# Hyena filters made ahead of the first norm, and half of them beside the second layer's norm, in a two-layer hybrid backbone on one core

## What is computed

```python
for l in range(DEPTH):                                   # DEPTH = 2
    ml = (silu(c) @ w_mod[l] + b_mod[l])                 # 6 modulation vectors of 1024, for c and c_ctx
    hl = modulate(rms_norm(xl, norm1_g[l]), ml[0], ml[1])
    p = hl @ w_in[l]                                     # one wide input projection
    # three mixers: neighbourhood attention, pooling, and the order-2 Hyena:
    #   hh = sin(freq * (z @ w1 + b1)); hh = sin(freq * (hh @ w2 + b2))
    #   hh = (hh @ w3).reshape(n, 2, 2, 512) * decay      (order, forward/backward)
    #   buf = concat(forward, 0, reversed backward); buf /= sum(abs(buf)); spectrum = rfft(buf)
    #   z = gate_o * irfft(rfft(z) * spectrum_o), for order o = 0, 1
    # merged by gates, projected, gated residual
    # then norm, router, top-2 of 16 experts, gated residual:
    xl = xl + ml[5] * f
out = rms_norm(xl, final_g)
```

## Time and profile before

| | us |
|---|---|
| median of three runs | 1842.62 |
| lowest, highest | 1838.25, 1848.77 |
| the profiled execution | 1845.94 |
| its span in the trace | 1844.2 |

### The profile page before, as it was taken

How to read it: one execution, slowest core, us unless ns; L and a number is a source line. 1 busy time by engine, 2 the same in 40 slices (tenths; PEclk the granted TensorE clock), 3 DMA queues, 4 the chain that set the end, 5 groups by cost and what they waited for, 6 DMA issues and landing times. The chain is left out here.

```text
span 1844.2 us, 19309 instructions
## 1 busy us (share of the span) xinstructions
PE 1546.9 (84%) x7556; PEld 1071.5 (58%) x7556; DVE 819.1 (44%) x1204; ACT 605.2 (33%) x830; POOL 357.9 (19%) x206
## 2 busy tenths in 40 slices
PE   5898997789999977999999766789889987777872
PEld 1365676556666646788888334468678973222322
DVE  2621666751111245889899444144853433000102
ACT  2322222351111242787877124122242331000002
POOL 0132332112222301101010112335124540000000
PEclk8799999799999986999999787889899997999996
DMA  7456321102242305899999722753205446999992
GB/s 247 134 206 239 124 65 52 43 1 69 68 137 68 114 25 217 323 405 405 408 407 368 292 87 83 295 183 99 73 10 179 161 138 229 420 421 422 422 398 80
DMA packets 118416, 374.29 MB, mean 203 GB/s; under 512 B 8222, under 2 KB 70880, under 8 KB 87360
## 3 DMA queue, kind: packets, MB, share of 16 engines
q1 hardware_dynamic: 107584, 334.58, 48.1%
q0 software_dynamic: 10752, 38.61, 5.5%
HBM read 356.39 MB, written 16.78 MB: 202 GB/s over the span
## 5 line engine op out<-in xcount | busy, mean ns | idle before, releaser
L587 POOL TENSOR_TENSOR w_lo<-ring,w_hi 128x1024 fp32r<-128x1024 f32 x120 | 288.7, 2418 | 724.0 <-ACT w_hi L1328 724.0
L705 PE MATMUL bank<-h_hi,w_hi 128*128 128x512 f32 (+1 forms) x896 | 329.8, 368 | 35.3 <-DVE h_lo L1609 21.2
L706 PE MATMUL bank<-h_hi,w_lo 128*128 128x512 f32 (+1 forms) x896 | 311.6, 348 | 0.0
L707 PE MATMUL bank<-h_lo,w_hi 128*128 128x512 f32 (+1 forms) x896 | 311.5, 348 | 0.0
L705 PEld LDWEIGHTS bank<-h_hi,w_hi 128*128 128x128 f32 x896 | 176.3, 197 | 84.9 <-issue 44.6
L706 PEld LDWEIGHTS bank<-h_hi,w_lo 128*128 128x128 f32 x896 | 177.0, 198 | 23.2 <-issue 5.0
L707 PEld LDWEIGHTS bank<-h_lo,w_hi 128*128 128x128 f32 x896 | 176.2, 197 | 20.2
L1328 ACT ACTIVATE w_hi<-ring 128x1024 fp32r<-128x1024 f32 x120 | 125.2, 1052 | 107.9 <-DMA ring<-in_w_in 76.1
L705 PE MATMUL bank<-w_hi,h_hi 128*128 128x512 f32 (+1 forms) x384 | 142.1, 370 | 9.8 <-DVE w_lo L1880 5.1
L1857 DVE SCALAR_TENSOR_TENSOR mix<-mix,bank 128x512 f32<-128x512 f32 (+1 forms) x48 | 26.6, 554 | 262.3 <-PE bank L985 165.4
L706 PE MATMUL bank<-w_hi,h_lo 128*128 128x512 f32 (+1 forms) x384 | 138.8, 362 | 0.0
(11 more groups left out here) (260 smaller groups left out, 2326.9 us busy)
## 6 DMA issues: line engine op xcount, KB each, us to landing
ring<-in_w_up_e SPq DMA_DIRECT2D x54, 1024.0 KB, 8.2
ring<-in_w_in SPq DMA_DIRECT2D x52, 1024.0 KB, 7.0
mix<-in_w_gate_e SPq DMA_DIRECT2D x52, 1024.0 KB, 8.4
ring<-in_w_mod SPq DMA_DIRECT2D x48, 1024.0 KB, 7.2
mix<-in_w_down_e SPq DMA_DIRECT2D x34, 1024.0 KB, 8.9
ring<-in_w_down_e SPq DMA_DIRECT2D x30, 1024.0 KB, 7.8
ring<-in_w_branch SPq DMA_DIRECT2D x12, 1024.0 KB, 5.2
ring<-in_w_gate_e SPq DMA_DIRECT2D x12, 1024.0 KB, 8.6
```

The source lines that it names most:

```text
L587: pool.tensor_tensor(w_lo[:, slot], rview(raw, 8)[:, :, x * P:(x + 1) * P], w_hi[:, slot].bitcast(F32), ALU.subtract).then_inc(w_l, 1)
L705: first = mm(dst, stat[0], mov[0], start=start, stop=False)
L706: mm(dst, stat[1], mov[0], start=False, stop=False)
L707: return first, mm(dst, stat[0], mov[1], start=False, stop=stop)
```

## The change

In the first layer the six tables that the filters need (`c_cols` and `par0` among them) are loaded first, with their own semaphore; `square` and `xT` follow, then the transform tables and the decay with a third semaphore, `s_lds`. TensorE makes `filter_in(0, 0)`, `filter_in(0, 1)` and `filters(0, 0)` ahead of the norm's sums. Then come the eight modulation chunks with `spectra_a(0, 0)` after the fourth, then the transposes of the modulation rows, and `spectra_b(0, 0)` behind them. The products of order 1 use bank 5 in place of bank 7 and have work areas of their own in the second layer (`late_fpm`, `late_fraw`, `late_fhid`). `spectra_a(0, 1)` comes after tile 1, `spectra_b(0, 1)` after tile 2.

Between the layers only order 0 is made ahead of the combination of expert rows; ScalarE takes the rows first and `spectrum_b` after them, and TensorE transposes the modulation rows ahead of `spectra_b`. `filters(1, 1)` stands ahead of the second layer's norm, `spectra_a(1, 1)` behind its sums, `spectra_b(1, 1)` after tile 0 of the projection; on VectorE `taps(1, 1)` stands ahead of the mean.

The diff, cut to its core:

```diff
-        fbank = [bank[i] for i in (2, 3, 4, 7)]
+        fbank = [[bank[i] for i in (2, 3, 4, x)] for x in (0, 5)]
...
-            for dst, name in ((cc[:, 0, :], "c_cols"), (square[:], "square"), (par[0][:], "par0"),
-                              (xT[:], "x_cols")):
-                sp.dma_start(dst, a[name]).then_inc(s_ld, 16)
...
+                if l == 0:
+                    sp.dma_start(cc[:, 0, :], a["c_cols"]).then_inc(s_ldf[l], 16)
+                    sp.dma_start(par[0][:], a["par0"]).then_inc(s_ldf[l], 16)
+                for dst, src in ((fz[l], a["filter_in"]), (fw1[l], a["hy_w1"][l]), (fw2[l], a["hy_w2"][l]),
+                                 (w3s[l], a["hy_w3"][l])):
                     sp.dma_start(dst, src).then_inc(s_ldf[l], 16)
                 if l == 0:
+                    sp.dma_start(square[:], a["square"]).then_inc(s_ld, 16)
+                    sp.dma_start(xT[:], a["x_cols"]).then_inc(s_ld, 16)
+                    sp.dma_start(dft_f[:], a["dft_f"]).then_inc(s_lds, 16)
+                    sp.dma_start(nyq[:], a["nyq"]).then_inc(s_lds, 16)
+                sp.dma_start(decay[l], a["decay"]).then_inc(s_lds, 16)
...
-            pe.wait_ge(s_ld, 16 * 4)
-            norm_pe(0, NT)
...
             def filters(l, o):
                 if o:
-                    pe.wait_ge(f_d[l], 10 * l + 6)
+                    pe.wait_ge(m_tk[l], 3 * l + 1)
                     pe.wait_ge(f_a[l], 6 * l + 4)
                 else:
                     pe.wait_ge(f_a[l], 6 * l + 2)
-                    pe.wait_ge(n_a, l + 1)
...
             def spectra_b(l, o):
                 pe.wait_ge(f_d[l], 10 * l + 5 + 4 * o)
+                if l == 0 or o:
+                    pe.wait_ge(n_a, 2 * l + 1)
...
-            def filters_and_mod(l):
-                filter_in(l, 0)
-                for k in range(DK):
+            def mods_and_filters(l, ks):
+                for k in ks:
                     mod(l, 0, k)
-                    if k == 1:
+                    if k == 1 and l:
                         filter_in(l, 1)
-                    elif k == 3:
+                    elif k == 3 and l:
                         filters(l, 0)
-                    elif k == 5:
+                    elif k == (5 if l else 3):
                         spectra_a(l, 0)
+                mod_columns(l, 0)
                 spectra_b(l, 0)
-                mod_columns(l, 0)
-                filters(l, 1)
+            filter_in(0, 0)
+            filter_in(0, 1)
+            filters(0, 0)
+            pe.wait_ge(s_ld, 16 * 2)
+            norm_pe(0, NT)
             pe.wait_ge(s_cs, 1)
-            filters_and_mod(0)
+            pe.wait_ge(s_lds, 16 * 3)
+            mods_and_filters(0, range(DK))
+            filters(0, 1)
...
                 if l:
+                    filters(l, 1)
                     norm_pe(2 * l, NT)
+                    spectra_a(l, 1)
...
-                    if l == 0 and g == 0:
+                    if l == 0 and g == 1:
                         spectra_a(l, 1)
-                    elif l == 0 and g == 1:
+                    elif g == (0 if l else 2):
                         spectra_b(l, 1)
...
-                    filters_and_mod(l + 1)
-                    spectra_a(l + 1, 1)
-                    spectra_b(l + 1, 1)
-                    pe.wait_ge(f_a[l + 1], 6 * l + 12)
-                    pe.wait_ge(f_d[l + 1], 10 * l + 20)
+                    filter_in(l + 1, 0)
+                    mods_and_filters(l + 1, range(DK))
+                    pe.wait_ge(f_a[l + 1], 6 * l + 10)
                     pe.wait_ge(m_tk[l + 1], 3 * l + 4)
...
                 for k in range(DK):
+                    if k == DK - 1 and l + 1 < DEPTH:
+                        pe.wait_ge(f_d[l + 1], 10 * l + 16)
...
-            act.wait_ge(s_ld, 16 * 4)
+            act.wait_ge(s_ldf[0], 16 * 6)
             A(cc[:, 1, :], cc[:, 0, :], ACT.Exp, scale=-1.0).then_inc(s_ce, 1)
-            norm_act_root(0, NT, 2)
             filter_sin(0, 0)
             filter_sin(0, 1)
+            act.wait_ge(s_ld, 16 * 2)
+            norm_act_root(0, NT, 2)
             spectrum_a(0, 0)
-            spectrum_b(0, 0)
             mod_rows(0, 0)
...
                 if l:
                     norm_act_root(2 * l, NT, 2)
+                    spectrum_a(l, 1)
+                else:
+                    spectrum_b(l, 0)
...
-                    act.wait_ge(z_r, 1)
-                    spectrum_b(l + 1, 0)
-                    spectrum_a(l + 1, 1)
-                    spectrum_b(l + 1, 1)
                 for j in range(nt):
                     act.wait_ge(z_g[j], 32 * (l + 1))
                     A(fa[:, j, :], fa[:, j, :], ACT.Copy, scale=wsel[:, 0, j:j + 1]).then_inc(z_s[l], 1)
+                if l + 1 < DEPTH:
+                    act.wait_ge(z_r, 1)
+                    spectrum_b(l + 1, 0)
...
             def taps(l, o):
                 dve.wait_ge(f_p[l], 8 * l + 3 + 3 * o)
+                dve.wait_ge(s_lds, 16 * (3 + l))
...
-            norm_dve_mean(0, NT)
             angle(0, 0)
-            norm_dve_root(0, NT)
             angle(0, 1)
             taps(0, 0)
-            gate_scales(0, 0)
+            norm_dve_root(0, NT)
             mod_first(0)
...
                 if l:
+                    taps(l, 1)
                     norm_dve_root(2 * l, NT)
                 norm_dve_scale(2 * l, NT)
                 if l == 0:
+                    gate_scales(0, 0)
                     taps(0, 1)
-                    gate_scales(0, 1)
...
+                    if g == (0 if l else 2):
+                        gate_scales(l, 1)
...
                     taps(l + 1, 0)
-                    gate_scales(l + 1, 0)
                     mod_first(l + 1)
-                    taps(l + 1, 1)
-                    gate_scales(l + 1, 1)
...
+                if l + 1 < DEPTH:
+                    gate_scales(l + 1, 0)
```

More of the change, by code:

```diff
@@ L755, in spectra_a @@
                     for j in range(2):
-                        mm(bank[2 + f][:], dft_f[:, j, f * P:(f + 1) * P], fpm[l][:, 0, j, :],
+                        mm(bank[2 + f][:], dft_f[:, j, f * P:(f + 1) * P], fpm[l][o][:, 0, j, :],
                            start=j == 0, stop=j == 1)
                 for j in range(2):
-                    last = mm(bank[4][0:1, :], nyq[:, j:j + 1], fpm[l][:, 0, j, :], start=j == 0, stop=j == 1)
+                    last = mm(bank[4][0:1, :], nyq[:, j:j + 1], fpm[l][o][:, 0, j, :], start=j == 0, stop=j == 1)
                 last.then_inc(f_p[l], 1)
```

41 lines of the change are left out of this document (20 added, 21 removed).

## The result

| | before, us | after, us |
|---|---|---|
| median (six runs each, side by side) | 1844.49 | 1830.29 |
| lowest, highest | 1838.25, 1848.77 | 1827.18, 1832.04 |
| the profiled execution | 1845.94 | 1831.84 |
| its span | 1844.2 | 1830.1 |

The ratio is 0.992, 95% interval 0.9898 to 0.9943: 14.2 us less. Forecast were 31 us less and 1800 to 1828; the measured median lies above that range. The direction was right, the size was not. What came is near rival 1, the cold start (1826).

What follows compares the result with a forecast made beforehand. Chains of short engine handovers ahead of both layers' input projections were taken as the bound. Savings of 12 us in the first layer and 18.7 (28.7 - 3.3 - 6.7) later gave 31, from 1842.62 to 1812, range 1800 to 1828.

Steps and rivals of the forecast that it cites:

- rival 1: Filters, norm, modulation and spectra in both layers run at TensorE's lower clock: gain only 17 us, time 1826; chance 0.14.
- The combination moves: Between the layers, combining expert rows ahead of the second spectrum starts the transposes at 1070.9 instead of 1099.61: 28.7 us less.
- Rival 2: Between the layers, something unnamed holds ScalarE or the gathered rows until 1090, so the combination stays: 1841 us; chance 0.04.
- The stall after tile 0 goes: First layer's projection: TensorE's 3.17 us wait for the second filter's taps and 1.5 us of slow clock disappear.
- What is late next in the first layer: The last modulation chunk's load, not the filters, becomes late: the eighth chunk lands at 52 to 56 us.
- The step from the columns at VectorE at about 56 to the first scaling at about 62.5: First layer: `spectra_b` (1.9 + 3.68 us) and its copies precede scaling, which starts 7.5 us earlier, bounds 4 and 10.
- That the second filter's products run beside the first scalings as before: First layer: these products, 3.6 to 7.2 us on TensorE, overlap the first scalings, as in the kernel before.
- `filters(1, 1)` ahead of the norm: Second layer: 3.6 us of products at the higher clock delay the mean by 3.3 us, bounds 3 and 8.
- `spectra_b(1, 1)` after tile 0: Second layer's projection: its products and ScalarE's copies delay the load loop's start by 6.7 us, upper bound 10.5.
- Rival 3: First layer's projection: spectra between tiles leave waits and half-speed tiles; slower from 6 tiles, 1856 with 8; chance 0.03.
- the price and its cover: First layer's scaling: VectorE and GpSimd's shared port costs up to 3 us, hidden while `spectra_b` holds ScalarE.

Runs made afterwards that it cites:

- joined: Changed kernel with second filter's products before the eighth modulation chunk, unused products before the fourth and before `filters(1, 1)`, `spectra_b(1, 1)` after tile 3: 1802.87 us.
- experiment 2: Changed kernel with four unused products added on TensorE ahead of both the fourth and the eighth modulation chunk of the first layer: 1820.16 us.
- Experiment 7: Changed kernel again (1830.4 us), with the second filter's products moved before the first layer's eighth modulation chunk (1820.47), and two kernels combining edits (1802.87, 1812.69).
- experiments 6: Changed kernel with eight unused products added before `filters(1, 1)` and ten behind `spectra_a(1, 1)`, between the layers: 1820.43 us.
- experiment 4: Changed kernel with `spectra_b(1, 1)`, its copies and scales after tile 3 of the second layer's projection instead of tile 0: 1813.16 us.
- warm and late: Changed kernel with four unused products ahead of the first layer's fourth and eighth modulation chunks, and `spectra_b(1, 1)` after tile 3: 1812.69 us.
- filters early: Changed kernel with the first layer's second filter products moved ahead of the eighth modulation chunk, using other banks: 1820.47 us.
- experiments 6 and 5: The latter: changed kernel with the second layer's order-1 filter products behind the norm's sums, taps behind the scaling, spectra after tiles 2 and 3: 1822.10 us.

## Why the forecast was too high, point by point

The step that failed is the pricing of TensorE's work behind waits. `spectra_b(0, 0)`, `filters(1, 1)` and `spectra_b(1, 1)` were entered with durations at 2.4 GHz and the first layer's second filter products at nothing; all ran at or near 1.2 GHz, and the second filter's products stood on the path. The move of the combination came as forecast.

**The combination moves: right.** Term 28.7. From the last expert stage to the residual `after` gains 28.3 less 0.6, 27.7; its second execution 27.8, `joined` 27.9. Rival 2 is refuted.

**The stall after tile 0 goes: right.** `spectra_a(0, 1)` has no wait for taps and takes 3.59 us at 90.07; in other kernels the wait is 0.3. The first projection product comes 3.5 us later than before, yet after the projection the kernel is 2.9 ahead: 6.4 us gained, where the term was 4.7.

**What is late next in the first layer: right in kind.** The fourth and eighth chunks each have a DMA wait; the eighth's product came at 56.56, just past the late edge of 52 to 56, beyond which the forecast called itself wrong.

**The step from the columns at VectorE at about 56 to the first scaling at about 62.5: wrong by 8 us.** The first scaling was at 70.32. 3.6 us of it stand ahead of the columns, which VectorE took at 59.57 (the norm's sums end at 34.94, forecast 31.5: they began 1.4 us late and took 10.04 at a mixed clock). 4 are `spectra_b` at or near 1.2 GHz, 9.6 us, for which I had taken 5.6. This is rival 1's mechanism, but in the first layer not its place. I had looked for the cold clock at the start of the run, where TensorE has done nothing; it came after both 3.4 us waits, the last of which I had forecast myself without asking what it does to the products behind it. The filled waits show this: the first scaling then starts at 61.94 to 64.23, about where the forecast had it, and by experiment 2's trace the first layer is 7 us better than the changed kernel's.

**That the second filter's products run beside the first scalings as before: wrong, the other error of reading.** They wait for `f_a` at 4, ScalarE's copies of the first filter's spectrum. Before, they too waited, but the columns stood behind the spectrum and gave them the time; now the columns come ahead, the scaling follows the copies at once, and the first projection product stands behind 6.5 us of filter. From the first scaling to the first product it was 3.4 us before, 6.7 after. Together with the clock this ate the 7.5 us of gain there; most of it is the clock again, for at 3.67 us the same stretch is 3.8 (table above). Experiment 7 puts them elsewhere.

**`filters(1, 1)` ahead of the norm: term mis-sized.** Taken 3.6 us, measured 7.19; with the norm's sums behind it at 8.64 the mean came 7.4 us later relative to the residual instead of 3.3. The reason given for 3.6 was that TensorE comes from transposes with a gap of some 2.5 us. The gap was 3.46 us. With the gap filled it is 3.70 and 3.4 (experiments 6 and 7). My upper bound, 8, had held.

**`spectra_b(1, 1)` after tile 0: term mis-sized, mechanism right.** Taken 6.7 us, measured 9.9, bound 10.5. Rival 1 had both of these terms, 7.2 for the filter's products and 9 for this spectrum (9.1 on TensorE). I took the higher clock behind a tile whose products wait for each scaled row. In experiment 4 the mean and the loop's start are equally far ahead, so the delay is gone with the move and the work shows up nowhere else.

**Sum.** Forecast by stages: 12, 28.7, -3.3, -6.7, 30.7. Measured: 0.6 (2.9 less 2.3 of a wandering clock), 27.7, -7.4, -9.9 and 3.4 again after the loop's start: 14.4. Of the 16 us missing some 11 are in the first layer (9 without the wandering) and 8 between the layers, and 3 came back. The misses weren't independent: one cause, the clock after a wait, sat in four terms of the sum, and I had put each at its good value, with a chance of 0.14 that all went the other way. A range to 1828 covers one or two of them. That rival 1's 1826 comes near the measured 1830.29 is in part luck: it had the norm's sums at 14 us, which took 10.04, and did not have the first layer's `spectra_b` and second filter. The Trainium skill, "TensorE: Matmul & The Clock Gate", Part 1, which the forecast used for rival 1, also says that the number of slow products varies from run to run of one kernel, and advises that the ramp costs under 1% and is not to be fitted. The traces agree with both: the eight products of `spectra_a(0, 0)` took 3.70 to 5.90 us in one and the same first layer (last section), and 10 us of 1830 is 0.5%. But where a change is worth 1.7%, 0.5% is a third of the forecast.

**Rival 3** (half speed over many tiles of the first layer's projection) did not come: from 80 us on the windows have the clock at 0.82 and then 1.00.

**Still open.** The changed kernel's two executions differ by 4.1 us in the first projection product (76.98 and 72.88), yet stand 2.9 and 2.4 us ahead after the first layer. TensorE's waits for ring chunks from 76 to 150 us are 4.5 and 5.2 us. So the ring takes back a part of a sooner start, but 0.7 isn't 4.1, and I have no run that tells the rest.

## What to carry to other kernels

A duration read at one clock holds at its new place only at that clock, and behind the second wait of the first layer (3.35 to 3.52 us) it was the lower one seven times of seven; so when a step is moved behind such a wait, cost everything up to the next dense stretch at the lower clock, and count this as one case for all terms that share it. Work that is free to move belongs into such a wait, where it costs nothing and can keep the clock, and not beside a chain's last step: of two places for the second filter's products, 19 us apart, one put 1.4 us on the path, or about 4 at the lower clock, and the other nothing. Filling makes the work right behind the wait fast; it promises nothing for what comes later (6.62 us in warm and late). And one trace of a kernel is one draw: compare several before a gain of 5 us is put down to an edit. In a loop bound by its own turn, put extra work after its loads are under way, and never ahead of the instruction that lets the first of them go.

## What the runs showed of the hardware that was not expected

One program, two behaviours. Behind a first wait of 3.37 us the changed kernel's `spectra_a` took 5.90 us, and the same instructions behind a wait of 3.19 us, in the kernel with late spectra, 3.70:

```profile
39.45 1.06 PE L730 MATMUL bank<-ring,csil 128*32 128x512 f32 x8 [3.19 <-DMA ring<-in_w_mod]
40.45 3.70 PE L760 MATMUL bank<-mix,dft_f 128*128 128x512 f32 x8
```

The length of the wait doesn't decide it: behind 3.31 and 3.35 us, in the kernels of experiments 6 and 5, the same eight products took 3.70 too, behind 3.36 us in the changed kernel's second execution 5.54, and behind 3.31 us in filters early 4.30. Behind its second wait, 3.38 us, the kernel with late spectra too went to 1.2 GHz (column sums 3.41). And the clock can stay down for long although the engine has work. Windows of the changed kernel about and after the mean:

```profile
1090.00:1102.00 12.00, 9.99 (x23) 3.19 (x22) 10.63 (x10) 5.52 (x8) 0.00 (x0) 1.00 0.00 0
1102.00:1122.00 20.00, 14.04 (x45) 10.61 (x46) 13.01 (x26) 10.30 (x18) 2.36 (x1) 0.50 0.00 1
```

In the second, which begins in a wait of 5.96 us, TensorE is busy 14.04 of 20 us, with tile 0 as its rows come and then without a pause, and stands at 0.50 all the time; in the 12 us before, busy 9.99, it had stood at 1.00. In the first layer it is busy 4.00 of 4 us from 60 to 64, at 0.50 too.

VectorE's first two multiplications beside GpSimd's subtractions took 3.44 us in `joined`, 1.28 in the changed kernel, where they began 0.75 us ahead of GpSimd's. In the changed kernel the third multiplication, begun at 63.52 us while GpSimd's subtractions still ran, took 2.83. The forecast had the price and its cover; the cover holds even where the spectrum is fast, for the first scaling, at 63.56, waits for ScalarE's copies:

```profile
57.35 3.44 DVE L1626 TENSOR_TENSOR mix<-xT,mix 128x512 f32<-128x512 f32 x2
57.59 5.40 POOL L594 TENSOR_TENSOR w_lo<-ring,w_hi 128x1024 fp32r<-128x1024 f32 x2 [56.99 <-ACT w_hi L1358]
...
63.08 0.57 ACT L1336 ACTIVATE mix<-bank 1x512 f32<-1x512 f32 x1
63.56 1.07 ACT L1290 ACTIVATE mix<-mix,mods,gs 128x256 f32<-128x256 f32 x2
```
